# Hybrid retention and window-attention trunk: low parts of block 0's attention weights moved among VectorE's steps, and the closing norm by half rows

## The reference

```python
def rmsnorm(x, g):
    xf = x.astype(jnp.float32)
    y = xf * lax.rsqrt(jnp.mean(xf * xf, axis=-1, keepdims=True) + EPS)
    return (y * g.astype(jnp.float32)).astype(x.dtype)
...
    q, g = jnp.split(proj, 2, axis=-1)
    q = apply_rope(q.reshape(B, S, SWA_HEADS, SWA_HEAD_DIM), cos, sin)
    s = jnp.einsum('bnqgrd,bnkgd->bngrqk', qc, kb).astype(jnp.float32) * (SWA_HEAD_DIM ** -0.5)
    m = jnp.maximum(jnp.max(s, axis=-1, keepdims=True), sink)
    p = jnp.exp(s - m)
    probs = p / (jnp.sum(p, axis=-1, keepdims=True) + jnp.exp(sink - m))
    o = jnp.einsum('bngrqk,bnkgd->bnqgrd', probs.astype(vb.dtype), vb)
    y = o * jax.nn.silu(g)
    return y @ w_out
...
    return rmsnorm(h, final_norm)
```

## Time and profile before

| what | value |
|---|---|
| median of 3 runs | 2431.52 us (2429.89 to 2432.43) |
| the profiled execution's own time | 2432.74 us |
| its span in the profile | 2431.0 us |
| mean granted TensorE clock | 0.999 |
| DMA | 625.85 MB, mean 257 GB/s |

### The profile page before, as it was taken

The page is one execution under the profiler, slowest core; times in us unless marked ns, Lnnn a source line. Parts: engine busy times, 40 slices in busy tenths (PEclk is TensorE's granted clock), DMA queues, the critical chain, the costliest instruction groups (busy, mean ns, idle before and its releaser), DMA issues.

```text
span 2431.0 us, 28657 instructions
## 1 busy us (share of the span) xinstructions
PE 2389.9 (98%) x11216; PEld 1963.4 (81%) x11216; DVE 1502.2 (62%) x2043; ACT 680.0 (28%) x1470; POOL 445.5 (18%) x323
## 2 busy tenths in 40 slices
PE   7999999999999999999999999999999999999998
PEld 6788888877887788888888888888888787888886
DVE  6554655567767767764767564564667645647384
ACT  2212212235221212232523121232352212313253
POOL 2111111221345655630010010100001101101000
PEclk9999999999999999999999999999999999999999
DMA  9667575654899999974379877775357977786433
GB/s 363 265 234 291 194 275 207 256 194 163 321 402 396 355 370 374 359 292 167 109 260 326 276 259 259 259 248 202 122 210 241 329 259 260 252 290 235 173 104 147
DMA packets 131978, 625.85 MB, mean 257 GB/s; under 512 B 8880, under 2 KB 9648, under 8 KB 110000
## 3 DMA queue, kind: packets, MB, share of 16 engines
q1 hardware_dynamic: 123008, 588.53, 67.0%
q10 hardware_dynamic: 8880, 36.18, 4.0%
HBM read 471.58 MB, written 153.09 MB: 257 GB/s over the span
## 4 chain that ended last, share of the span: by engine, by line
PE 90%; DVE 6%; DMA 1%; issue 1%; ACT 0%; POOL 0%; SPq 0%; DVEq 0%; ACTq 0%
PE ps L721 29%; PE ps L723 28%; PE ps L722 28%; PE ps L1236 2%; DVE ff L2311 1%; PE ps L1246 1%; DMA raw<-in_stream 1%; PE ps L1044 1%; DVE fr L1695 1%; PE ps L874 1%; DMA whl<-split_w 1%; DVE mx L2351 1%; DVE xlo L1695 0%; DVE ff L2381 0%; PE ps L1176 0%
## 5 line engine op out<-in xcount | busy, mean ns | idle before, releaser
L721 PE MATMUL ps<-whl,xhi 128*128 128x512 f32 (+1 forms) x1088 | 416.6, 383 | 2.3 <-DVE xlo L1695 2.3
L723 PE MATMUL ps<-whl,xlo 128*128 128x512 f32 (+1 forms) x1088 | 411.5, 378 | 0.0
L722 PE MATMUL ps<-whl,xhi 128*128 128x512 f32 (+1 forms) x1088 | 410.4, 377 | 0.0
L721 PE MATMUL ps<-xhi,whl 128*128 128x512 f32 x768 | 304.3, 396 | 16.5 <-DVE xlo L1699 13.3
L723 PE MATMUL ps<-xhi,whl 128*128 128x512 f32 x768 | 300.4, 391 | 0.0
L722 PE MATMUL ps<-xlo,whl 128*128 128x512 f32 x768 | 299.9, 390 | 0.0
L721 PE MATMUL ps<-whl,fr 128*128 128x512 f32 x640 | 256.7, 401 | 4.3 <-DVE whl L1737 2.1
L723 PE MATMUL ps<-whl,fr 128*128 128x512 f32 x640 | 254.1, 397 | 0.0
L722 PE MATMUL ps<-whl,fr 128*128 128x512 f32 x640 | 253.4, 396 | 0.0
L721 PEld LDWEIGHTS ps<-whl,xhi 128*128 128x128 f32 x1088 | 204.9, 188 | 40.2 <-issue 3.1
L723 PEld LDWEIGHTS ps<-whl,xlo 128*128 128x128 f32 x1088 | 204.7, 188 | 38.6
(11 more groups left out here) (218 smaller groups left out, 3839.6 us busy)
## 6 DMA issues: line engine op xcount, KB each, us to landing
whl<-split_w SPq DMA_DIRECT2D x60, 2048.0 KB, 8.4
whl<-split_w SPq DMA_DIRECT2D x118, 1024.0 KB, 6.9
split_w<-whl SPq DMA_DIRECT2D x44, 2048.0 KB, 7.2
whl<-vg_w SPq DMA_DIRECT2D x64, 1024.0 KB, 6.8
raw<-in_stream SPq DMA_DIRECT2D x43, 1024.0 KB, 9.4
vg_w<-ff SPq DMA_DIRECT2D x32, 1024.0 KB, 9.6
whl<-comb_w SPq DMA_DIRECT2D x32, 1024.0 KB, 6.4
raw<-in_stream SPq DMA_DIRECT2D x52, 512.0 KB, 10.1
```

Of the source, the lines that this page charges most:

```text
L721: pe.matmul(dst, lhs[0], rhs[0], start=start, stop=False)
L722: pe.matmul(dst, lhs[0], rhs[1], start=False, stop=False)
L723: return pe.matmul(dst, lhs[1], rhs[0], start=False, stop=stop)
```

## The change

Four edits in block 0's attention, and one at the program's end.

- Chunk 3 is split in two parts, one before the rotation of query tile 1, one before that of tile 2.
- In the steps, part 1 of chunk 7 moves from the end of step 3 to step 6, behind the rotation and ahead of the probabilities; chunks 9 and 10 are split whole at the end of steps 10 and 12, not in parts over two steps.
- Part 0 of chunk 7 signals a new semaphore, on which TensorE's first half of gate tile 4 waits; the second half waits for the whole chunk.
- In the last block, the squares and the multiplication by the norm weight of column half 0 are done while TensorE works on column half 1. Behind each addition of half 1 only that half is squared; the mean square adds both sums; VectorE scales half 1 (512 columns) and ScalarE half 0, and ScalarE stores a tile before it turns to the next root.

```diff
-STEP_PARTS = {0: (6, (0, 1)), 2: (7, (0,)), 3: (7, (1,)), 7: (8, (0,)), 8: (8, (1,)), 10: (9, (0,)), 11: (9, (1,)),
-              12: (10, (0,)), 13: (10, (1,)), 15: (11, (0,)), 16: (11, (1,))}
+STEP_PARTS = {0: (6, (0, 1)), 2: (7, (0,)), 7: (8, (0,)), 8: (8, (1,)), 10: (9, (0, 1)), 12: (10, (0, 1)), 15: (11, (0,)), 16: (11, (1,))}
...
                     c = GATE_CHUNK[f]
-                    if half == 0 and GATE_CHUNK[f - 1] != c:
+                    if first and f == 4:
+                        if half == 0:
+                            pe.wait_ge(gate_part.sem, 1)
+                        else:
+                            w_wait(at, c)
+                    elif half == 0 and GATE_CHUNK[f - 1] != c:
                         w_wait(at, c)
...
+            def close_rows(at):
+
+                def square_half(n, t):
+                    act.wait_ge(h2_add.sem, at(h2_add, 4 * n + t + 1))
+                    cols = slice(n * 512, (n + 1) * 512)
+                    to, done = ((tail_sq[:, t:t + 1], tail_sum), (ssq[:, t:t + 1], sq_sum))[n]
+                    act.activation(squares[:, t, cols], hres[:, t, cols], ACT.Square, accum_out=to).then_inc(done.sem, 1)
+
+                def store_tile(t):
+                    act.wait_ge(tail_scaled.sem, t + 1)
+                    act.wait_ge(fin.sem, at(fin, t + 1))
+                    act.dma_start(out[(BLOCKS - 1) * BT + t * P:(BLOCKS - 1) * BT + (t + 1) * P, :], hres[:, t, :]).then_inc(out_stored.sem, 16)
+
+                for t in range(TT):
+                    square_half(0, t)
+                for t in range(TT):
+                    square_half(1, t)
+                    if t > 0:
+                        store_tile(t - 1)
+                    act.wait_ge(tail_gained.sem, t + 1)
+                    act.wait_ge(rstd_done.sem, at(rstd_done, 2 + t))
+                    act.activation(hres[:, t, 0:512], hres[:, t, 0:512], ACT.Copy, scale=rstd[:, t:t + 1]).then_inc(tail_scaled.sem, 1)
+                store_tile(TT - 1)
...
-            def split_chunk(n, parts=(0, 1)):
+            def split_chunk(n, parts=(0, 1), done=None):
...
                 if parts[-1] == 1:
                     ins.then_inc(w_ready[n % 2].sem, 16)
+                elif done is not None:
+                    ins.then_inc(done.sem, 1)
...
                 for t in range(TT):
-                    if first and t == 1:
-                        split_chunk(n0 + 3)
+                    if first and t in (1, 2):
+                        split_chunk(n0 + 3, (t - 1,))
                     rope_q(0, t)
...
                     if 3 <= s < 7:
                         rope_q(1, s - 3)
+                    if first and s == 6:
+                        split_chunk(n0 + GATE_CHUNK[4], (1,))
...
                     if first and s in STEP_PARTS:
-                        split_chunk(n0 + STEP_PARTS[s][0], STEP_PARTS[s][1])
+                        split_chunk(n0 + STEP_PARTS[s][0], STEP_PARTS[s][1], gate_part if s == 2 else None)
...
+                def gain_half(t):
+                    dve.wait_ge(tail_sum.sem, t + 1)
+                    if t == 0:
+                        dve.wait_ge(fn_loaded.sem, at(fn_loaded, 1))
+                    dve.tensor_tensor(hres[:, t, 0:512], hres[:, t, 0:512], fn[:, 0:512], ALU.mult).then_inc(tail_gained.sem, 1)
+
                 for t in range(TT):
                     add_to_h2(0, t)
                     if not last:
                         next_lo(at, 8, 4 + t)
+                    elif t > 0:
+                        gain_half(t - 1)
+                if last:
+                    gain_half(TT - 1)
+                    dve.tensor_scalar(tail_sq[:, :], tail_sq[:, :], 1.0 / D, EPS, ALU.mult, ALU.add).then_inc(tail_gained.sem, 1)
+                    dve.wait_ge(tail_gained.sem, TT + 1)
...
-                        dve.tensor_scalar(ms[:, t:t + 1], ssq[:, t:t + 1], 1.0 / D, EPS, ALU.mult, ALU.add).then_inc(ms_done.sem, 1)
-
-                    add_to_h2(1, 0)
...
-                    norm_tile(b, 3, 5)
+                        dve.scalar_tensor_tensor(ms[:, t:t + 1], ssq[:, t:t + 1], 1.0 / D, tail_sq[:, t:t + 1],
+                                                 ALU.mult, ALU.add).then_inc(ms_done.sem, 1)
+
+                    def norm_half(t):
+                        dve.wait_ge(rstd_done.sem, at(rstd_done, 2 + t))
+                        dve.scalar_tensor_tensor(hres[:, t, 512:D], hres[:, t, 512:D], rstd[:, t:t + 1], fn[:, 512:D],
+                                                 ALU.mult, ALU.mult).then_inc(fin.sem, 1)
+
+                    for t in range(TT):
+                        add_to_h2(1, t)
+                        if t > 0:
+                            norm_half(t - 1)
+                        mean_square_of(t)
+                    norm_half(TT - 1)
```

More of the change, by code:

```diff
@@ L146, in build @@
         ssq = sb("ssq", [P, 4])
+        tail_sq = sb("tail_sq", [P, 4])
         rstd = sb("rstd", [P, 4])
@@ L237, in build @@
         lead_ready = count("w_lead_ready")
+        gate_part = count("w_gate_first_half_ready")
         w_stored = [count(f"w_stored{i}", head=4, post=7, unit=16) for i in range(2)]
@@ L258, in build @@
         sq_sum = count("sq_sum", post=8)
+        tail_sum = count("tail_sq_sum")
+        tail_gained = count("tail_gained")
+        tail_scaled = count("tail_scaled")
         ms_done = count("mean_squares", post=2)
@@ L1679, in one_block @@
                     next_hi(at, 0)
-                square_sums(at, True)
                 if last:
-                    store_out(b)
+                    close_rows(at)
+                else:
+                    square_sums(at, True)
             one_block(0, True, False)
@@ L2441, in mean_square_of @@
                         dve.wait_ge(sq_sum.sem, at(sq_sum, 5 + t))
-                        dve.tensor_scalar(ms[:, t:t + 1], ssq[:, t:t + 1], 1.0 / D, EPS, ALU.mult, ALU.add).then_inc(ms_done.sem, 1)
-                    add_to_h2(1, 0)
-                    add_to_h2(1, 1)
-                    mean_square_of(0)
-                    add_to_h2(1, 2)
-                    mean_square_of(1)
-                    dve.wait_ge(fn_loaded.sem, at(fn_loaded, 1))
-                    norm_tile(b, 0, 2)
-                    add_to_h2(1, 3)
-                    mean_square_of(2)
-                    norm_tile(b, 1, 3)
-                    mean_square_of(3)
-                    norm_tile(b, 2, 4)
-                    norm_tile(b, 3, 5)
+                        dve.scalar_tensor_tensor(ms[:, t:t + 1], ssq[:, t:t + 1], 1.0 / D, tail_sq[:, t:t + 1],
[10 more added lines that the diff above has]
+                    norm_half(TT - 1)
             one_block(0, True, False)
```

## The result

| kernel | median | range | ratio to before, 95% interval |
|---|---|---|---|
| before (runs of this comparison) | 2430.7 us | 2429.72 to 2432.43 | |
| after | 2419.25 us | 2415.79 to 2419.57 | 0.9945 [0.9933, 0.9957] |

The forecast was 2424.5, in a range of 2421.8 to 2427.6. The kernel became faster by 11.45 us, by more than the range allowed. The ratio is not the quotient of the two medians, which is 0.9953 and lies within its interval. The profiled execution of after took 2415.79 us, the fastest of its four, which is 16.95 less than the 2432.74 of the profiled one of before; so the two traces show more than the medians do.

A forecast was written before the change was run, and what follows sets the result against it. TensorE, busy 98% of the span, was taken to bound the kernel. Gains of 1.3 + 4.3 + 1.9 = 7.5 us gave 2425.2 from the profiled 2432.74, 2424.0 by the median; stated 2424.5, range 2421.8 to 2427.6.

The forecast's parts named there:

- 1.3 + 4.3 + 1.9 = 7.5: Whole kernel: gains in us from chunk 3's split, block 0's 16 steps and the closing norm, added up.
- (C): Closing norm at the program's end: half-row work lets the last store go earlier, gain 1.9 us, bounds 1.5 and 2.3.
- (A): Before block 0's steps: half of chunk 3's low parts ahead of the second rotation, gain 1.3 us, bounds 1.1 and 1.6.
- (B): Block 0's 16 attention steps: moved chunk splits bring step 15's scores 4.3 us earlier, bounds 2.6 and 5.65.
- the wait: forecast 2.65 us: Near step 14: GpSimd's rounding hits VectorE's negated maximum or sum; TensorE waits 2.65 us for step 11's low probabilities.
- rival 1: Block 0's late steps: GpSimd's rounding misses VectorE's small operations, wait 1.3 us, total gain 8.85 us; chance 17%.
- Step 8's scores: 550.6 instead of 552.27: Block 0, step 8: TensorE's scores start at 550.6 us instead of 552.27, after chunk 7's second half moved to step 6.
- rival 2: Block 0's late steps: TensorE's clock falls anyway after the 2.65 us wait, costing 1.7 us, total gain 5.8; chance 18%.
- Rivals 3, 4 and 5: Steps pass wait on, total ≤4.9 us (12%); ScalarE's queue bounds the end, 5.6 us (5%); slower, chunk 9's load late (3%).
- the 1.57 us: Block 0: chunk 7's second half, 1.57 us on VectorE, leaves step 3 and returns in step 6; full return feared at 12%.

The follow-up runs named there:

- steps_only: Kernel before with the four edits in block 0's attention alone, old closing norm, old tile placement: 2429.14 us, ratio 0.9985.
- best: Kernel after, fr and fx 64 bytes higher, ScalarE's last query store (step 7) and result copies (steps 11, 13, 14) ahead of exponentials: 2410.41 us, ratio 0.991.
- after_q: Kernel after with ScalarE's last store of rotated queries in block 0 ahead of step 7's exponentials: 2417.09 us, ratio 0.9937.
- tail_only: Kernel before with only the closing norm by half rows, tail_sq declared last so fr stays at its old place: 2432.18 us, ratio 0.9996.
- shift32: Kernel before with one unused tile that puts fr, ff and fx 32 bytes higher, no instruction changed: 2423.93 us, ratio 0.9962.
- shift64: Kernel before with one unused tile that puts fr and fx 64 bytes higher, nothing else changed: 2431.53 us, ratio 0.9994.
- fr_only: Kernel before with fr 32 bytes higher and the tile of fx and ff 64 bytes higher: 2424.36 us, ratio 0.9968.
- chunk7_only: Kernel before with only part 1 of chunk 7 moved to step 6, with the semaphore for its first half: 2431.36 us, ratio 0.9997.
- after_384: Kernel after with an unused tile of 80 floats ahead of fr, moving fr and fx up: 2411.69 us, ratio 0.9913.
- all_up_32: Kernel after with fr and fx 64 bytes higher, then every large tile another 32 bytes higher: 2411.29 us, ratio 0.9913.
- all_up_128: Kernel after with fr and fx 64 bytes higher, then every large tile another 128 bytes higher: 2411.09 us, ratio 0.9912.

## Why the prediction missed

**What failed.** The step is in the sum, "1.3 + 4.3 + 1.9 = 7.5": it takes the edits alone, and lets all else cost what it did. The diff has a new tile in the list of declarations, as far as (C) needs it (`tail_sq`), and I gave its place no line, neither a price nor "nothing, because". It was the largest term: 7.8 us by the ratios, 5.5 by the medians, 9.3 by the spacings. No rival had it, so the range was too narrow for a cause outside the stages. The trace of before held half a warning: with the same shape, and `whl` streamed in both, products that load `xhi` or `xlo` follow each other in 0.2278 us and those that load `fr` in 0.2334 us, a difference that nothing in the code explains.

**(A)** Forecast 1.3, bounds 1.1 and 1.6. From tile 0's transposes to step 0's scores it took 505.55 - 474.81 = 30.74 us before and 502.03 - 472.49 = 29.54 after: 1.2. Right; at the third tile 0.3 us were to come back, and 0.15 did.

**(B)** Forecast 4.3 to step 15's scores (bounds 2.6 and 5.65); measured 3.67 in after, 3.6 in steps_only at the old place. Right in sign, place and within the bounds: no wait for low parts is left, and the one wait near step 14 came at the values. Two of its steps were off. Timelines of PE, DVE, ACT and POOL in after:

```profile
580.40 0.47 PE L725 MATMUL ps<-fr,vwin 128*128 128x512 f32 x1 [1.61 <-ACT ff L1668]
...
574.88 2.28 DVE L1771 TENSOR_TENSOR whl<-raw,whl 128x2048 fp32r<-128x2048 f32 x1
577.80 0.16 DVE L2391 SCALAR_TENSOR_TENSOR nm<-mx,nsink 128x4 f32<-128x4 f32 x1
578.68 2.44 DVE L1729 TENSOR_TENSOR fr<-ff,fr 128x512 fp32r<-128x512 f32 x2
...
578.00 0.37 ACT L1682 ACTIVATE ff<-ps,nm 128x128 f32<-128x128 f32 x1 [2.19 <-DVE nm L2391]
579.48 0.78 ACT L1668 ACTIVATE ff<-ps 64x256 f32<-64x256 f32 x2
...
578.08 1.90 POOL L631 TENSOR_SCALAR whl<-raw 128x2048 fp32r<-128x2048 f32 x1 [8.46 <-PE ps L727]
```

First, the wait: forecast 2.65 us, measured 1.61. GpSimd's rounding missed the negated maximum and hit the low parts of the attention output, where nobody waited. That is the condition of rival 1, whose wait was 1.3 us, though its total was not reached. What is left of the wait has another cause than I gave: the exponentials stood behind chunk 10's whole split and the maximum, and ScalarE's copy (L1668), which frees the bank for the next values, behind the exponentials; it ended at 580.26, and TensorE went on at 580.40. I had followed VectorE's queue past the moved split and not ScalarE's. Removing that order in best moved the start of the output product by only a part, since the low parts of the attention output were next.

The Trainium skill ("SBUF — State Buffer", section "Who interferes with whom") says that a VectorE instruction with two SBUF inputs contends with a GpSimd instruction that reads SBUF; the trace agrees, with 2.44 us for two operations that take 1.28 alone.

Second, "Step 8's scores: 550.6 instead of 552.27": they came at 551.73 on the same clock (548.21 + 3.52, the difference of the two starts of step 0's scores), a gain of 0.54 and not 1.67. The 1.1 us were still missing at step 13's scores (576.34 against the 575.25 that 4.75 us a step give); the shorter wait returned a part of it. Chunk 7's second half now delays step 7's row maximum, through it the exponentials, and behind those stands the store of the last rotated query tile, for which the scores of step 8 wait 0.90 us: again ScalarE's queue. after_q shows that this cost nothing in the end. So it is in part luck that 3.67 lies so near 4.3: the two errors, 1.1 us too late at step 13 and a wait 1.0 us too short, go against each other.

**(C)** Forecast 1.9; measured 8.1 - 6.2 = 1.9 in after and the same in tail_only.

**The rivals.** The clock (rival 2) was not put to the test in after, whose longest wait there is 1.61 us; the granted clock stayed at 1.00. It fell behind 2.1 us in before, shift32, shift64, fr_only and tail_only, and not behind the same 2.1 us in chunk7_only. So its price is real (1.5 us, by the one pair of before and chunk7_only; the forecast had 1.7) but it isn't decided by the length of the idle time alone. The Trainium skill ("TensorE: Matmul & The Clock Gate", section "What's actually happening") has the window run free of the program; five falls behind six like waits agree with that, without showing it. Rivals 3, 4 and 5 did not happen: the 1.57 us did not come back in full, ScalarE was not late at the end, and no wait for chunk 9's load is in the trace.

## What to carry to other kernels

A new tile is an edit of every tile declared behind it: before a change is priced, work out which large operands move, and declare small new tiles last when the edit itself is to be measured. Where TensorE is busy all the time, compare the spacing of equal matmuls that differ only in the tiles they read; a few nanoseconds times two thousand is more than a stage's tuning, and an unused tile of some bytes is a one-line trial. When a long operation is moved on one engine, follow the queues of the engines that its neighbours release, to the buffers that they free.

## What the runs showed of the hardware that was not expected

How fast matmuls in the reduced-precision float32 format follow each other depends on how the tile of the stationary operand lies to others. With 512 streamed columns it is from 0.2276 us at distance 0 to 0.2334 us at 64 and 160 bytes modulo 256 and 0.2333 at 224, 2.5%; 256 more bytes change nothing (after_384), nor does moving all tiles together (all_up_32, all_up_128). The Trainium skill ("TensorE: Matmul & The Clock Gate", section "Step-by-step: what each phase is for") says that loading the next weights doesn't take read bandwidth from the running matmul. If the partner is the tile of split weights, streamed while the next part of `fr` is loaded, these runs speak against that as a rule for every placement; which tile it is, no run here shows. Products that load `whl` itself and stream `xhi` and `xlo`, whose places never moved against each other, kept 0.2273 to 0.2278 us in every trace.
